# One decoder layer on one core: the output projection in three passes of split operands

## The reference

```python
merged = (gates[:, :, 0] * (y_attn @ w_proj_attn[l])
          + gates[:, :, 1] * (y_pool @ w_proj_pool[l])
          + gates[:, :, 2] * (y_mem @ w_proj_mem[l]))
h = h + merged @ w_out[l]
h = h + moe(rmsnorm(h, norm_ffn_g[l]), w_router[l], b_router[l], w_up[l], b_up[l],
            w_down[l], b_down[l])
```

## Time and profile before

| | |
|---|---|
| median of 3 runs | 1215.26 us (1214.33 to 1217.21) |
| span of the profiled execution | 1214.7 us |
| PE busy | 1131.6 us (93%) |
| DVE busy | 359.5 us (30%) |
| ACT busy | 227.4 us (19%) |
| POOL busy | 128.5 us (11%) |
| read from HBM | 441.65 MB, 364 GB/s over the span |

### The profile page before, as it was taken

One profiled execution on the slowest core, in us unless ns is written; L12 is line 12 of the kernel. 1 busy time (PEld: TensorE's weight loads), 2 busy tenths in 40 slices (PEclk: granted clock), 3 DMA queues, 4 the chain that ended last, 5 costly groups with the idle time before them and its releaser, 6 DMA issues.

```text
span 1214.7 us, 14754 instructions
## 1 busy us (share of the span) xinstructions
PE 1131.6 (93%) x5609; PEld 506.6 (42%) x5609; DVE 359.5 (30%) x766; ACT 227.4 (19%) x415; POOL 128.5 (11%) x59
## 2 busy tenths in 40 slices
PE   6899999989999999999999979999999899999996
PEld 5788899753333333233333323323222233222222
DVE  4593664632222222122223212222222122222222
ACT  5344554121111111111111111111111111111112
POOL 5562566300000000000000000000000000000000
PEclk9999999989999999999999989999999999999999
DMA  9554235779999999999999999999999999999993
GB/s 355 188 188 147 95 139 190 302 315 359 423 421 421 421 422 419 420 421 421 421 421 421 421 420 421 421 421 421 422 421 421 420 421 422 421 421 421 421 421 145
DMA packets 77890, 444.33 MB, mean 366 GB/s; under 512 B 9166, under 2 KB 12664, under 8 KB 28664
## 3 DMA queue, kind: packets, MB, share of 16 engines
q1 hardware_dynamic: 75904, 441.65, 88.9%
q10 hardware_dynamic: 1912, 1.66, 0.5%
HBM read 441.65 MB, written 1.05 MB: 364 GB/s over the span
## 4 chain that ended last, share of the span: by engine, by line
PE 55%; DMA 19%; SPq 15%; DVE 5%; ACT 3%; issue 3%; POOL 0%; DVEq 0%; ACTq 0%
PE psum L1472 21%; SPq L459 15%; PE psum L1173 11%; PE psum L1508 11%; DMA ring<-in_w_up 9%; DMA gate_area<-in_w_up 5%; DMA qk_area<-in_w_up 4%; PE psum L1427 3%; PE psum L1360 2%; DVE gate_area L1110 1%; DVE gate_area L1106 1%; DVE gate_area L1104 1%; PE psum L1495 1%; ACT gate_area L766 1%; PE psum L1481 1%
## 5 line engine op out<-in xcount | busy, mean ns | idle before, releaser
L1472 PE MATMUL psum<-ring,gate_area 128*64 128x512 f32 x1312 | 311.4, 610 | 28.4 <-DMA ring<-in_w_up 18.4
L1076 DVE TENSOR_TENSOR h_s<-psum,h_s 128x512 f32<-128x512 f32 x132 | 82.0, 683 | 433.2 <-PE psum L1427 433.2
L1472 PEld LDWEIGHTS psum<-ring,gate_area 128*64 128x64 f32 x1312 | 90.2, 139 | 234.5 <-issue 170.6
L1508 PE MATMUL psum<-ring,gate_area 128*64 128x512 f32 x640 | 145.8, 595 | 5.3 <-ACT gate_area L766 5.3
L531 POOL TENSOR_TENSOR unit_lo<-ring,unit_hi 128x1024 fp32r<-128x1024 f32 (+1 forms) x54 | 128.1, 2377 | 95.5 <-ACT unit_hi L564 95.4
L760 ACT ACTIVATE gate_area<-gate_area 128x512 f32<-128x512 f32 x32 | 20.1, 629 | 545.5 <-DVE gate_area L1102 545.5
L1102 DVE TENSOR_SCALAR gate_area<-psum 128x512 f32<-128x512 f32 x32 | 22.1, 692 | 283.5 <-PE psum L1481 283.5
L1508 PEld LDWEIGHTS psum<-ring,gate_area 128*64 128x64 f32 x640 | 44.4, 136 | 86.2 <-issue 76.9
L1427 PE MATMUL psum<-pT_s,gate_area 64*128 64x512 f32 x264 | 65.6, 615 | 0.7 <-ACT pT_s L770 0.7
L564 ACT ACTIVATE unit_hi<-ring 128x1024 fp32r<-128x1024 f32 (+1 forms) x54 | 55.5, 1032 | 47.5 <-PE psum L1173 47.4
L1408 PE MATMUL psum<-xn_area,gate_area 128*64 128x512 f32 x264 | 63.8, 604 | 0.4 <-DVE gate_area L1048 0.4
(11 more groups left out here) (256 smaller groups left out, 1229.1 us busy)
## 6 DMA issues: line engine op xcount, KB each, us to landing
ring<-in_w_up SPq DMA_DIRECT2D x164, 1024.0 KB, 26.5
ring<-in_w_down SPq DMA_DIRECT2D x80, 1024.0 KB, 26.9
gate_area<-in_w_up SPq DMA_DIRECT2D x16, 1024.0 KB, 27.0
xT_area<-in_w_up SPq DMA_DIRECT2D x16, 1024.0 KB, 27.1
ring<-in_w_gate SPq DMA_DIRECT2D x6, 2048.0 KB, 8.7
qk_area<-in_w_up SPq DMA_DIRECT2D x12, 1024.0 KB, 26.5
mem_s<-in_w_up SPq DMA_DIRECT2D x12, 1024.0 KB, 28.2
yl_area<-in_w_up SPq DMA_DIRECT2D x12, 1024.0 KB, 26.9
```

Source lines behind the costliest of these rows:

```text
L1076: nc.vector.tensor_tensor(h_s[:, b, cols], psum[:, BACK_BANKS[j], :], h_s[:, b, cols], ALU.add).then_inc(added, 1)
L1472: ins = nc.tensor.matmul(psum[lo:lo + SLOTS, c, :], lhsT, w[:, at:at + 512], start=(k == 0), stop=False)
L1508: ins = nc.tensor.matmul(psum[c * SLOTS:(c + 1) * SLOTS, DOWN_BANK, :], lhsT, w[:, at:at + 512], start=(f == 0), stop=(f == KC - 1))
```

## The change

Merged rows and `w_out` are now split into a high and a low part, and the output projection makes three fp32r passes per chunk instead of one float32 product. `w_out` becomes eight more units (O0 and O1, four each). Both token blocks of a column half are filled together, unit by unit. The transposes of the first half stand behind the first unit of the second half, and router products go by halves.

```diff
+UNITS += [(f"O{hf}", "rows", j) for hf in range(2) for j in range(KC // 2)]
...
-            sp.wait_ge(bank_filled, FILLED["gate", 3 * KC - 1])
-            load(0, 11, 11)
...
             sp.wait_ge(bank_filled, FILLED["br", KC - 1, 2])
-            for q in range(8, 11):
-                load(0, q, q)
             sp.wait_ge(got_parts, 24 * 16)
             load(1, 1, 13)
             sp.wait_ge(merged_ready, KC)
             load(1, 2, 14)
             load(1, 6, 18)
             for name in ("O0", "O1"):
-                sp.wait_ge(bank_filled, LAST_USE[name])
+                sp.wait_ge(lo_ready, LAST_SPLIT[name])
                 load_over(name)
+            sp.wait_ge(bank_filled, FILLED["out", B - 1, 1])
+            for q in range(8, 12):
+                load(0, q, q)
             load(1, 0, 12)
...
-            for u in range(22 + 3 * KC + UNIT_SLOTS, len(UNITS)):
+            for f in range(KC):
+                split(P_UNIT + UNIT_SLOTS + f)
+                act.wait_ge(merged_ready, f + 1)
+                nc.scalar.activation(merged_hi[:, f, :], merged[:, f % 2, :], ACT.Copy).then_inc(merged_hi_ready, 1)
+            act.dma_start(wr_s, rows(w_router[0])).then_inc(got_router, 16)
+            for u in range(O_UNIT + UNIT_SLOTS, len(UNITS) - 2):
                 split(u)
...
             copy_x2T(0, 0)
+            split(len(UNITS) - 2)
+            copy_x2T(1, 0)
+            split(len(UNITS) - 1)
+            nc.scalar.activation(warm[:], eps_s[:], ACT.Sqrt)
+            act.wait_ge(dve_emptied, EMPTIED["out", 0, 1])
+            squares_of(h_s, 16, 0)
             copy_x2T(0, 1)
...
+            def take_merged_lo(f):
+                dve.wait_ge(merged_hi_ready, f + 1)
+                nc.vector.tensor_tensor(merged_lo[:, f, :], merged[:, f % 2, :], merged_hi[:, f, :].bitcast(F32),
+                                        ALU.subtract).then_inc(merged_lo_ready, 1)
+                dve.wait_ge(merged_lo_ready, f + 1)
+
...
-                nc.vector.tensor_tensor(merged[:, f, :], mix_t[:, 0, :], mix_t[:, 2, :], ALU.add)\
+                nc.vector.tensor_tensor(merged[:, f % 2, :], mix_t[:, 0, :], mix_t[:, 2, :], ALU.add)\
                   .then_inc(merged_ready, 1)
                 dve.wait_ge(merged_ready, f + 1)
+                if f > 0:
+                    take_merged_lo(f - 1)
+            take_merged_lo(KC - 1)
...
-            for b in range(B):
-                for hf in range(2):
+            for hf in range(2):
+                for b in range(B):
...
+            def out_unit(t, hf, j):
+
+                hi, lo = next_unit()
+                for b in range(B):
+                    for i in range(2):
+                        k = 2 * j + i
+                        if hf == 0 and b == 0:
+                            pe.wait_ge(merged_lo_ready, k + 1)
+                        s = slice(b * P, (b + 1) * P)
+                        ins = three_passes(t[b], (merged_hi[:, k, s], merged_lo[:, k, s]), (hi[:, i, :], lo[:, i, :]),
+                                           k == 0, k == KC - 1)
...
+            t = [fill(("out", b, 0)) for b in range(B)]
+            for j in range(KC // 2):
+                out_unit(t, 0, j)
+            t = [fill(("out", b, 1)) for b in range(B)]
+            out_unit(t, 1, 0)
             turn_h(0, 0)
-            turn_h(0, 1)
-            project_out(1, 1)
+            turn_h(1, 0)
+            for j in range(1, KC // 2):
+                out_unit(t, 1, j)
             t_logits = fill("logits")
             pe.wait_ge(got_router, 16)
...
+            logits(0, 0)
+            logits(1, 0)
+            turn_h(0, 1)
             turn_h(1, 1)
-            done(logits(1))
+            logits(0, 1)
+            done(logits(1, 1))
```

## The result

The changed kernel takes 1220.15 us (median of 5 runs, 1219.15 to 1221.22) against 1215.26, a difference of 4.9. The ratio estimated from the runs is 1.0038 with a 95% interval of 1.0026 to 1.005: 4.6 us slower, between 3.2 and 6.1. The profiled execution of after has a span of 1218.3 us. The device time is not the span: in the 24 runs of before that have both on record it is 2.2 to 2.3 us longer, in the five of after 1.7 to 1.9. An execution of before with a span of 1214.7 thus has a device time near 1217, which is near the upper end of its range and not 0.6 under the median, as the prediction took it. The forecast adds a difference to the median, so nothing in it hangs on this.

A forecast was written before the change was run, and what follows sets the result against it. TensorE's path through branches and projection was taken to delay the DMA-bound expert loop. Passes save 5.7 us, but the ring ends the projection 4.9 us later, the rest unchanged: 1215.26 + 4.9 = 1220.2 us, range 1212.5 to 1226.

The forecast's parts named there:

- The ring: Branch stage: GpSimd's subtraction, VectorE's additions and ACT's splits delay each other in a circle; 4.65 us per chunk against 2.91.
- the block: Branch stage: GpSimd's subtraction keeps VectorE's operations with two SBUF inputs out for 2.26 us from its start.
- Passes: Output projection: 96 fp32r products take 21.8 us instead of 27.5, 5.7 us shorter on TensorE alone.
- Waits for units: Projection's first half: TensorE waits about 1.9 us per unit for GpSimd's low parts, from 228 to 247 us.
- Second half: Projection's second column half: the third unit's split stands behind ACT's copy of the first transposes, a wait of about 1 us.
- Projection end: The output projection ends at 262.7 us instead of 257.8, 4.9 us later.
- From there to the first release: Projection end to the loop's first free slot: 20.2 us unchanged, with 1.6 us less as lower bound.
- The stream: Weight pieces ahead of the loop: again twelve before the projection's end and seven after; nothing gained or lost.
- The router load: Issued at 243.2 us, needed at 262.7, taken as hidden; landing after 22.2 us again would cost 2.7 us.
- the ring doesn't close: Rival, chance 0.19: VectorE's additions are not held, the projection ends 4.9 us earlier than before; about 1210 us.
- Closes in part: Rival, chance 0.10: some chunks escape the block, each giving back 1.7 us; 1214 to 1217 us.
- The clock falls: Rival, chance 0.07: two projection units run at 1.2 GHz, each taking 2.7 us more; about 1225 us.

The follow-up runs named there:

- e3: The changed kernel with gated products and merged chunk kept in PSUM, so no VectorE operation of the branch stage has two SBUF inputs: 1210.93 us.
- e7: e3 with the first half's transposes and their copies put back behind the projection's last unit: 1208.95 us.
- e2: The changed kernel with two added 128x256 ACT copies behind each chunk's high copy: 1216.97 us.
- e1: The changed kernel with one added 128x256 ACT copy behind each chunk's high copy: 1220.93 us.
- e5: The changed kernel with each ACT split one chunk earlier, ahead of the wait for the merged chunk: 1221.54 us.
- e8: e3 with the last two splits each one place earlier on ACT, ahead of the copies of the first half's transposes: 1212.14 us.

## Why the prediction was right, step by step

- **The ring closed** and the block is what it was priced at. It began where the prediction had it: the low subtraction of chunk 0 lost to GpSimd, and merged 2 ended 13.2 us after the start (13.3 predicted). In after, GpSimd starts at 226.69 and the held addition ends at 229.33: less 0.42 of own work it began 2.22 us after that start, 2.26 predicted. The period is 4.59 against 4.65, merged 7 at 36.17 after the start against 242.8 - 206.16 = 36.6. GpSimd is ready 1.49 us after a merged chunk (1.5). The prediction's sign "about 2.7 us from chunk 2 on" does not fit its own sum, which gives 1.5 + 2.26 + 0.43 - 1.6 = 2.6 and 1.5 for chunk 2; measured are 2.5 and 1.52. By the rule of the Trainium skill, "SBUF — State Buffer", section Who interferes with whom, the exclusion is right in every case seen here (e3 the cleanest), but a block of GpSimd's whole 2.37 would end 0.15 us later than the trace shows.
- **Passes**: 5.7 us shorter on TensorE alone. e7 confirms it: its projection ends 51.68 - 45.12 = 6.6 us earlier, of which 0.9 are the transposes that stood inside before.
- **Waits for units**: 1.3 to 1.8 us of idle each from 228 to 248, 1.9 predicted. A record outlasts the start of the next, so the fitting measure is the distance between the starts of the first half's units (4.30, 4.57, 4.75) less 2.72 of work: 1.6 to 2.0. The unit behind the router load's issue was ready at 40.2 us after the start, 247.1 - 206.16 = 40.9 predicted.
- **Second half**: the third unit waited 0.23 us instead of 1. The step missed a wait ahead of it: the transposes wait 0.51 us for VectorE's second multiplication with the gain, which stands behind the first, and that one is held to 2.69 us by GpSimd. The two make 0.7, nearly what was taken.
- **Projection end**: +4.6 against +4.9.
- **From there to the first release** the size was off: 19.25 us instead of 20.2, most of the way from "unchanged" towards the lower bound. Two terms of 1.6 us had been set against each other. The sixteen products ahead of the last transposes took 1.71, as reckoned, but the last eight ran at the upper clock, 0.14 each (the clock fell only at 270 us), so that 3.25 - 1.09 = 2.2 were saved and not 1.6. With 1.4 us more ahead of them on the path, the way to the last router product took 5.8 us instead of 6.6. The other 0.1 lies behind it and is the difference of two: from the gathering's first matmuls to the loop's first it took 6.22 us instead of 5.97, and from there to the twentieth piece 2.88 instead of 3.26, at a mean granted clock of 0.65 against 0.58. So counted from the start of the stage the twentieth piece is 3.7 us later, not 4.9. The runs say 4.6 to 4.9 with an interval of 3.2 to 6.1, which holds both. No trace places the rest of about 1 us, so that the forecast met the median to 0.1 us is partly chance.
- **The stream**: twelve pieces before and seven after, no pause, as worked out. **The router load** landed after 13.4 us, hidden.
- **Rivals**: "the ring doesn't close" happens only where it is taken apart (e3), and then on the predicted side: 1210.93, predicted about 1210. "Closes in part" is e2, 1216.97, at the upper end of its 1214 to 1217; every second chunk escaped, and 1.6 us of that went to the clock. "The clock falls" did not happen in after but in e1, e2 and e5, with 1.6 us once, not 2.7 twice.

The change as a whole: passes -5.7, ring and late units +10.3 (4.6 + 5.7), tail -0.9. The 5.7 is the price worked out above, the 0.9 is measured from the end of the projection to the twentieth piece, and the 10.3 is what is left. Most of it is not inherent in the split operands: e3 takes 9.1 of it away. The move of the transposes costs 0.8 where VectorE is not held (e7 against e3); in the changed kernel itself that was not tried.

## What to carry to other kernels

Before a subtraction goes to GpSimd, list the VectorE operations with two SBUF inputs in the same stretch, and ask whether a chain leads from GpSimd's result back to them. In the ring measured here chunks 3 to 7 each paid 2.1 us of a GpSimd instruction of 2.4. Splits one chunk earlier (e5) left the period as it was, one copy more (e1) only changed which operation was held, two copies more let every second chunk through (e2), and operands in PSUM ended it (e3). A stage of which TensorE was the bound has to be checked for its feeders' period (here 2.88 against 4.6), not their busy share: none of VectorE, ACT or GpSimd was over 31% of the span. All of this was measured in one kernel.

## What was not expected of the hardware

- Work added on an engine in the ring made the program faster: 1216.97 us with two extra copies per chunk on ACT against 1220.15 without, of which 1.8 us are seen in the stage.
- Neither engine starved the other here: with back-to-back GpSimd halves VectorE's waiting operation got in between each time (1.44 us), delaying the second half from 1.29 to 1.48 us.
- A wait of 1.99 us was followed by about 3.4 us at the lower clock in e1 (worked out from its windows), one of 1.74 us by none in after, and one of 2.22 us by none in e2.
- The branch stage starts 206.07 to 209.81 us into the trace though its instructions are the same. In e8 the whole difference to e3 is there by 62 us (the pooling products start at 62.48 against 60.03 in e3); its cause stays open. It is as large as the effects measured here, so the distance from the start of the stage tells more than one span.
- The router load landed after 22.2, 13.4 and 7.1 us in before, after and e1, with other pieces in flight.
